# First attention: values of two heads on the two halves of the array, products once per two query tiles, result feature-major

## The reference

```python
def forgetting_attention(q, k, v, f_logit, b_forget):      # 16 heads of 64
    log_f = log_sigmoid(f_logit + b_forget)
    cum = transpose(cumsum(log_f, axis=1), (0, 2, 1))
    for qb in range(4):                                    # query tiles of 128
        s = einsum('bqhd,bkhd->bhqk', q[:, qs:qe], k[:, :qe]) / 8
        s = s + (cum[:, :, qs:qe, None] - cum[:, :, None, :qe])
        p = softmax(where(s_pos <= t_pos, s, -inf))
        outs.append(einsum('bhqk,bkhd->bqhd', p, v[:, :qe]))

o = forgetting_attention(...)
y_att = o.reshape(B, S, 1024) @ w_att_out
m = sigmoid(g_conv) * y_conv + sigmoid(g_att) * y_att
x = x + m @ w_out
```

## Time and profile before

| | |
|---|---|
| median of 3 runs | 1786.18 us (1785.49 to 1787.08) |
| profiled execution | 1786.99 us, its span 1784.9 us |
| TensorE busy | 1715.3 us of the span (96%) |
| VectorE busy | 849.3 us (48%) |
| ScalarE busy | 639.0 us (36%) |
| mean granted TensorE clock | 0.987 |
| first attention, first scores to last product | 274 to 512 us |

### The profile page before, as it was taken

The page is one execution under the profiler, slowest core; times in us unless marked ns, Lnnn a source line. Parts: engine busy times, 40 slices in busy tenths (PEclk is TensorE's granted clock), DMA queues, the critical chain, the costliest instruction groups (busy, mean ns, idle before and its releaser), DMA issues.

```text
span 1784.9 us, 21909 instructions
## 1 busy us (share of the span) xinstructions
PE 1715.3 (96%) x8597; PEld 1251.2 (70%) x8597; DVE 849.3 (48%) x1578; ACT 639.0 (36%) x1102; POOL 96.3 (5%) x131
## 2 busy tenths in 40 slices
PE   6999999999999889999999998899999999999899
PEld 5888888888888744343434433788788888988677
DVE  3544345444565443333333334872647643447782
ACT  4122225444541401111111113754353332457760
POOL 0000001001000000000000000110011000000320
PEclk9999999999999889999999999999999999999999
DMA  6666364653216769999999996233023342313101
GB/s 151 88 102 97 106 95 72 63 62 66 71 64 246 262 265 425 426 427 426 427 427 428 426 426 269 83 118 95 24 71 95 95 151 82 108 59 98 49 1 71
DMA packets 111350, 317.55 MB, mean 178 GB/s; under 512 B 6485, under 2 KB 79957, under 8 KB 98448
## 3 DMA queue, kind: packets, MB, share of 16 engines
q1 hardware_dynamic: 108080, 309.57, 52.6%
q0 software_dynamic: 2160, 3.92, 0.6%
q10 hardware_dynamic: 1008, 2.65, 0.4%
HBM read 313.78 MB, written 6.30 MB: 179 GB/s over the span
## 4 chain that ended last, share of the span: by engine, by line
PE 88%; DVE 4%; ACT 3%; DMA 3%; issue 1%; SPq 0%; DVEq 0%; ACTq 0%; POOL 0%; POOLq 0%
PE bank L1403 14%; PE bank L1405 14%; PE bank L1404 14%; PE bank L1713 11%; PE bank L1739 6%; PE turned L1403 4%; PE turned L1405 4%; PE turned L1404 4%; PE bank L1484 2%; DMA up<-in_w_e_up 2%; PE bank L1586 2%; PE bank L1781 1%; PE turned L1484 1%; PE bank L1726 1%; DMA w_raw<-in_w_in 1%
## 5 line engine op out<-in xcount | busy, mean ns | idle before, releaser
L2031 DVE TENSOR_TENSOR w_lo<-w_raw,w_hi 128x2048 fp32r<-128x2048 f32 (+1 forms) x72 | 156.9, 2179 | 276.7 <-ACT w_hi L887 276.5
L887 ACT ACTIVATE w_hi<-w_raw 128x512 fp32r<-128x512 f32 (+3 forms) x138 | 169.7, 1252 | 284.2 <-DMA w_raw<-in_w_in 99.0
L1713 PE MATMUL bank<-gate,xt 128*64 128x512 f32 x512 | 225.8, 594 | 1.8 <-DMA up<-in_w_e_up 1.8
L1714 PE MATMUL bank<-up,xt 128*64 128x512 f32 x512 | 225.9, 594 | 0.0
L1713 PEld LDWEIGHTS bank<-gate,xt 128*64 128x64 f32 x512 | 68.7, 137 | 140.1 <-issue 140.1
L1403 PE MATMUL bank<-h1T_hi,w_hi 128*128 128x512 f32 x376 | 151.1, 402 | 0.0
L1405 PE MATMUL bank<-h1T_hi,w_lo 128*128 128x512 f32 x376 | 147.4, 392 | 0.0
L1404 PE MATMUL bank<-h1T_lo,w_hi 128*128 128x512 f32 x376 | 146.8, 390 | 0.0
L1739 PE MATMUL bank<-down,hT 128*64 128x512 f32 x256 | 118.3, 605 | 8.8 <-DVE hT L2360 8.8
L887 ACT ACTIVATE y_s<-bank,slot_w 64x512 f32<-64x512 f32 x63 | 43.0, 682 | 220.3 <-PE bank L1740 99.2
L1740 PE MATMUL bank<-down,hT 128*64 128x512 f32 x256 | 118.3, 605 | 0.0
(11 more groups left out here) (704 smaller groups left out, 3863.1 us busy)
## 6 DMA issues: line engine op xcount, KB each, us to landing
down<-in_w_e_down SPq DMA_DIRECT2D x32, 2048.0 KB, 24.1
up<-in_w_e_up SPq DMA_DIRECT2D x30, 2048.0 KB, 26.6
gate<-in_w_e_gate SPq DMA_DIRECT2D x30, 2048.0 KB, 21.6
w_raw<-in_w_in SPq DMA_DIRECT2D x24, 1024.0 KB, 9.7
w_raw<-in_a_w_in SPq DMA_DIRECT2D x20, 1024.0 KB, 5.3
w_raw<-in_w_in SPq DMA_DIRECT2D x16, 512.0 KB, 9.6
w_raw<-in_a_w_out SPq DMA_DIRECT2D x8, 1024.0 KB, 5.0
w_raw<-in_w_conv_out SPq DMA_DIRECT2D x4, 1024.0 KB, 4.9
```

The costliest lines, as they stand in the source:

```text
L887: return nc.scalar.activation(out, in_, ACT.Copy, scale=scale)
L1713: g_ins = pe.matmul(out[0:CAP, :], x, ring_gate[p][:, c, :], start=c == 0, stop=c == KC - 1)
L1714: u_ins = pe.matmul(out[CAP:, :], x, ring_up[p][:, c, :], start=c == 0, stop=c == KC - 1)
L2031: V.tensor_tensor(ring_view(w_lo, n), ring_view(raw, n), ring_view(w_hi, n).bitcast(F32), ALU.subtract)\
```

## The change

Items are counted in another order: two heads of a pair alternate, query tile by query tile (`head_of`, `tile_of`). The probabilities are scaled by VectorE in SBUF, right after exp, and the transposes wait for that (`p_normed`). Every fourth item TensorE does the value products of the last four items (two query tiles of both heads): stationary are 64 columns of `v1`, moving the 128 columns of `pT`; head 0 of the pair writes partitions 0 to 63 of bank 5, head 1 partitions 64 to 127, and bank 5 collects all four query tiles of a pair, feature-major. ScalarE copies the bank to `o1T` once per pair. There are seven `pT` buffers instead of two. The 32 transposes `OT1` are gone; high and low parts are made from `o1T` in SBUF, after the plan.

```diff
--- before.py
+++ after.py
@@ -161,6 +161,16 @@
     return plan
 
 
+def head_of(i):
+
+    return 2 * (i // 8) + i % 2
+
+
+def tile_of(i):
+
+    return i % 8 // 2
+
+
 def outputs_in_order():
 
     o = [("hT", 0, j) for j in range(KC)]
...
@@ -340,7 +348,7 @@
         f_one = temp("f_one", 11, (H1, 512))
         neg = temp("neg", 0, dt=F32R)
         p_t = [temp(f"p_t{b}", b) for b in (1, 2, 3, 4)]
-        pT_t = [temp(f"pT_t{b}", 5 + b, (P, TT, P)) for b in range(2)]
+        pT_t = [temp(f"pT_t{b}", 5 + b, (P, TT, P)) for b in range(7)]
 
         ring_gate = [big("gate0", 4), big("gate1", 2), at("gate2", [P, KC, FE], F32, BASE)]
         ring_up = [big("up0", 5), big("up1", 3), at("up2", [P, KC, FE], F32, BASE + BIG)]
...
@@ -644,6 +652,13 @@
             count = eng.value_load(over[0:1, 16:17], min_val=0, max_val=OVF)
             return count, lambda i: eng.value_load(over[0:1, bass.ds(i, 1)], min_val=0, max_val=NE - 1)
 
+        o1_left, o1_right, o1_copied, o1_split = sem("o1_left"), sem("o1_right"), sem("o1_copied"), sem("o1_split")
+
+        def until_o1(eng, m):
+
+            eng.wait_ge(o1_left, m + 1)
+            eng.wait_ge(o1_right, m + 1)
+
         moe_first = order[("hT", 1, 0)]
 
         def moe_drained(b):
...
@@ -697,7 +712,7 @@
                                  allow_slow_non_contiguous=True).then_inc(sem("gain_row_made"), 16)
                 if n == slice_no[("mix_out", 0, 0)]:
 
-                    until_taken(sp, ("OT1", KC - 1))
+                    sp.wait_ge(o1_split, KC)
                     sp.dma_start(x1_tok[:, :, :], x_v).then_inc(x_back, 16)
                     sp.wait_ge(sem("gain_row_made"), 16)
                     sp.dma_start(g_ffn[:, :], gain_dram.rearrange("d o -> o d").to_broadcast([P, D])).then_inc(sem("g_ffn_loaded"), 16)
...
@@ -1001,16 +1016,14 @@
             split(slice_no[("v1", 0)] + 2, slices1)
             q1_high(0)
             k1_high(0)
-            for i, _, done, now, pt, _ in plan:
+            for i, _, done, now, pt, o in plan:
                 for key, q in now:
                     split_piece(slice_no[key], q)
                 if i is not None:
-                    keys = (i % TT + 1) * P
+                    keys = (tile_of(i) + 1) * P
                     act.wait_ge(sem("max1_made"), i + 1)
                     if i >= 4:
                         act.wait_ge(results, order[("PT1", i - 4)] + 1)
-                    if i >= 8:
-                        until_taken(act, ("O1", i - 8))
                     took(nc.scalar.activation(p_t[i % 4][:, 0:keys], bank_of(("S1", i))[:, 0:keys], ACT.Exp,
                                               bias=neg_max[:, i % 8:i % 8 + 1], accum_out=row_sum[:, i % 8:i % 8 + 1]), ("S1", i))
                 for key in done:
...
@@ -1024,11 +1037,14 @@
                         src = until_made(act, key)
                         took(copy(gattT[:, key[1], :], src[:, :]), key)
                 if pt is not None and pt % 2 == 0:
-                    keys = (pt % TT + 1) * P
+                    keys = (tile_of(pt) + 1) * P
                     src = until_made(act, ("PT1", pt))
-                    if pt >= 2:
-                        act.wait_ge(results, order[("O1", pt - 2)] + 1)
-                    took(copy(pT_t[0][:, 0:pt % TT + 1, :], src[:, 0:keys].rearrange("p (k q) -> p k q", q=P)), ("PT1", pt))
+                    if pt >= 7:
+                        until_o1(act, (pt - 7) // 4 * 2 + 1)
+                    took(copy(pT_t[pt % 7][:, 0:tile_of(pt) + 1, :], src[:, 0:keys].rearrange("p (k q) -> p k q", q=P)), ("PT1", pt))
+                if o is not None and o % 8 == 7:
+                    until_o1(act, o // 2)
+                    copy(o1T[:, o // 8, :], bank[5][:, :]).then_inc(o1_copied, 1)
             split(slice_no[("att_out", 1)], slices1)
 
             def attention(n_items, S, PT, O, p_buf, pT_buf, bias_made, scale, among):
...
@@ -1054,7 +1070,8 @@
                                                   bias=b_, scale=s_, accum_out=row_sum[:, i % 8:i % 8 + 1]), (S, i))
 
             for j in range(KC):
-                evict_hi(("OT1", j), o1T_hi[:, j, :])
+                act.wait_ge(o1_copied, j + 1)
+                copy(o1T_hi[:, j, :], o1T[:, j, :]).then_inc(hi_made, 1)
             for j in range(KC):
                 until_taken(act, ("gatt", j))
                 nc.scalar.activation(gattT[:, j, :], gattT[:, j, :], ACT.Sigmoid).then_inc(sem("gatt_made"), 1)
...
@@ -1574,24 +1591,30 @@
                 for key, g in here:
                     dense_group(key, g)
                 if pt is not None:
-                    until_taken(pe, ("S1", pt))
-                    transposes(("PT1", pt), [(p_t[pt % 4][:, b * P:(b + 1) * P], P) for b in range(pt % TT + 1)])
-                if o is not None:
-                    if o % (4 * TT) == 0:
+                    pe.wait_ge(sem("p_normed"), pt + 1)
+                    transposes(("PT1", pt), [(p_t[pt % 4][:, b * P:(b + 1) * P], P) for b in range(tile_of(pt) + 1)])
+                if o is not None and o % 4 == 3:
+                    j = o // 8
+                    if o % 16 == 3:
                         for tp in range(2):
-                            until_taken(pe, ("v1", o // (4 * TT), tp))
-                    out = open_bank(pe, ("O1", o))
-                    until_taken(pe, ("PT1", o))
-                    for b in range(o % TT + 1):
-                        ins = pe.matmul(out[:, 0:HD1], pT_t[o % 2][:, b, :], v1[:, b, (o // TT) * HD1:(o // TT + 1) * HD1],
-                                        start=b == 0, stop=b == o % TT)
-                    ins.then_inc(results, 1)
-            for i in range(H1 * TT - 8, H1 * TT):
-                until_taken(pe, ("O1", i))
-            for j in range(KC):
-                transposes(("OT1", j), [(o1_tok[:, tt, j * P:(j + 1) * P], P) for tt in range(TT)])
+                            until_taken(pe, ("v1", o // 16, tp))
+                    if o == 3:
+                        pe.wait_ge(drained[5], len([k for k, (at_, _) in place_of.items() if at_ == 5 and order[k] < order[("S1", 0)]]))
+                    elif o % 8 == 3:
+                        pe.wait_ge(o1_copied, j)
+                    for i in range(o - 3, o + 1):
+                        until_taken(pe, ("PT1", i))
+                    for qt in (tile_of(o) - 1, tile_of(o)):
+                        for b in range(qt + 1):
+                            for x in range(2):
+                                h = 2 * j + x
+                                ins = pe.matmul(bank[5][half_rows(x), qt * P:(qt + 1) * P], v1[:, b, h * HD1:(h + 1) * HD1],
+                                                pT_t[(8 * j + 2 * qt + x) % 7][:, b, :], start=b == 0, stop=b == qt)
+                                if b == qt:
+                                    ins.then_inc((o1_left, o1_right)[x], 1)
+            pe.wait_ge(o1_copied, KC)
             for s in range(4):
-                feature_major("att_out", s, lambda j: ("att_out", j), o1T_hi, o1T_lo, chunk_taken("OT1"))
+                feature_major("att_out", s, lambda j: ("att_out", j), o1T_hi, o1T_lo, lambda c: pe.wait_ge(o1_split, c + 1))
             def turn_x1(h, tt):
                 until_taken(pe, ("mix_out", h, tt))
                 transposes(("h2T", h, tt), [(x1_tok[:, tt, (4 * h + c) * P:(4 * h + c + 1) * P], P) for c in range(4)])
...
@@ -2187,13 +2210,20 @@
             split(slice_no[("v1", 0)] + 2, slices1)
             q1_low(0)
             k1_low(0)
+            n_normed = 0
             for i, _, done, now, pt, o in plan:
                 if i is not None:
                     src = until_made(dve, ("S1", i))
                     if i >= 8:
                         until_taken(dve, ("S1", i - 8))
-                    V.tensor_reduce(neg_max[:, i % 8:i % 8 + 1], src[:, 0:(i % TT + 1) * P], AX_X, ALU.max, negate=True)\
+                    V.tensor_reduce(neg_max[:, i % 8:i % 8 + 1], src[:, 0:(tile_of(i) + 1) * P], AX_X, ALU.max, negate=True)\
                         .then_inc(sem("max1_made"), 1)
+                if i != 0 and (i is not None or pt is not None) and n_normed < H1 * TT:
+                    until_taken(dve, ("S1", n_normed))
+                    step(V.reciprocal(inv_sum[:, n_normed % 8:n_normed % 8 + 1], row_sum[:, n_normed % 8:n_normed % 8 + 1]))
+                    p_ = p_t[n_normed % 4][:, 0:(tile_of(n_normed) + 1) * P]
+                    V.tensor_scalar(p_, p_, inv_sum[:, n_normed % 8:n_normed % 8 + 1], None, ALU.mult).then_inc(sem("p_normed"), 1)
+                    n_normed += 1
                 for key, q in now:
                     split_piece(slice_no[key], q)
                 for key in done:
...
@@ -2203,16 +2233,11 @@
                         k1_low(key[1])
                 if pt is not None and pt % 2 == 1:
                     src = until_made(dve, ("PT1", pt))
-                    if pt >= 2:
```

(18 more changed lines are left out.)

14 lines of the change are left out of this document (6 added, 8 removed).

## The result

| | before | after |
|---|---|---|
| median us (runs) | 1786.63 (1785.49 to 1787.82, 4) | 1772.58 (1772.10 to 1773.57, 4) |
| ratio, 95% interval | | 0.9923 (0.9911 to 0.9936) |
| profiled execution, us | 1786.99 | 1772.31 |
| its span, granted clock | 1784.9, 0.987 | 1770.2, 0.985 |

The kernel after is 14.1 us (0.77%) faster. The forecast was 7.8 us faster, 1778.4, and the range ended at 1773.0, 0.4 us above the measured time. The sign and the mechanism held; the gain was taken too small.

The account below looks back on a forecast made before the run. TensorE was taken as the bound. Products, visits and old waits gain 10.9 us, less 0.5 of new waits and 2.6 in the tail: 7.8 faster, 1778.4 us (65%), range 1773 to 1784.

Parts of the forecast that it names:

- the price of before's products: First attention, TensorE value products: 12.6% of 239 us, 30.1 us for 320 records; 29.0 without the last item.
- A pair, 0.11: New value products on two array halves: both run at once, 0.11 us per pair, 146 pairs 16.1 us.
- A visit, 0.34: Going to the array halves and back: 0.20 out and 0.15 in, 0.34 us together; 15 visits 5.1 us.
- Waits: TensorE in the first attention: eight waits of 3.1 us go; 0.5 us of new ones in the last pair of heads.
- The old eight: Gaps before value products in the kernel before, waiting on bank 5 or ScalarE's copy; 3.1 us together.
- The tail: Last transposes to att_out: 8.9 us against 8.78, then 5 us at half clock costing 2.5; 2.6 us lost.
- Halves in turn: Rival for the value products: halves don't overlap, a pair costs 0.22 us; 9.7 us slower, 1795.9; 7%.
- Visits cost nothing: Rival for the value products: visits free and pairs 0.107 us; 13.4 us faster, 1772.8; 13%.
- The hand-over in VectorE: Rival: VectorE's chain late (2 us of waits), visits 0.5 us, clock low twice as long; 3.0 faster, 1783.2; 15%.

Follow-up runs that it names:

- the run with four items per visit: Kernel before, with a head's four query tiles' value products done together every fourth item, old whole-array form, seven pT buffers; 1785.64 us, ratio 0.9992.
- the kernel where VectorE scales first: Kernel before, with VectorE's scaling of the value product, which frees bank 5, ahead of the low parts of q and k; 1783.08 us, ratio 0.9982.
- slice split first: Kernel after, with ScalarE's high parts of the second att_out weight slice made ahead of its last copy of bank 5; 1766.65 us, ratio 0.9889.
- one half: Kernel after, with both heads' products sent to the same half of the array and partitions 0 to 63 of bank 5; 1790.01 us, ratio 1.002.
- both runs on the order of halves: Kernel after, value products head by head instead of alternating: within each query tile, 1776.69 us; within each whole visit, 1782.86 us.

## Why the prediction was right in kind and short in size

- **The step that failed: the price of before's products.** "The chain by line in that window gives the value products (L1586) 12.6%, 239 x 0.126 = 30.1 us" took the chain's share as the price of all 320 records. A chain gives a line only the time that the chain itself spends there, and at six places it runs through ScalarE and VectorE (k_high and k_low in the earlier trace rows) while TensorE works on. One of them, chain of before:

```profile
347.86 0.25 PE bank L1405
...
348.13 0.03 ACT k_high L887
...
352.80 0.41 PE bank L1586 x2
```

and the timeline of the same window, with a whole visit that the chain passes by:

```profile
348.04 1.00 PE L1586 MATMUL bank<-v,pT_t 128*128 128x64 f32 x8
```

  Piece by piece, 46 of the 320 records are left out at these six places. The 30.2 us belong to the other 274, 0.110 each, the price that doubling them measured (33.6 us for 306). So 306 records cost 33.7 us by the chain's own price, not 29.0. With the table's count it is 30.1 and the 5.0 in the transposes' row, 35.1. That is 6.1 of the 7.1 us by which the stretch was short. Of the 1.4 between 33.7 and 35.1, 1.2 would be passages to the products, 62 times the 0.02 of the run with four items per visit. That the table also shows 30.1 for the value products is chance: it is another count, start to start, over 306 records. The forecast had the sign of this in its own text: 0.105 per record times 320 is 33.6, and I took the smaller number without asking why they differ. (It also left the six records of item 62 in the stream, though the tail is counted from the transposes ahead of them: 0.7 us the other way.)
- **A pair, 0.11: right.** 0.109 in after, in the doubled products and in visits of every size. 146 pairs are 15.9 us.
- **A visit, 0.34: right.** 0.16 + 0.18 here, from an expert stage of another shape. The Trainium skill's rule (TensorEngine Tiling (Array Packing), Key Properties) that a change of tiling mode drains TensorE agrees with these numbers. The size was near by luck in part: the forecast took it from products of 512 columns and it had no baseline for what a passage costs without the change of mode (0.08 in before). Products and visits of after together: 18.2 + 15 x 0.17 = 20.8, forecast 21.2; that is 0.4 more of the difference.
- **Dense products took 0.7 us less.** Not forecast. It is spread over the 406 of 512 columns in the body of the groups, under 0.003 us each; why stays open.
- **Waits: right.** The old eight are gone, 3.1 by the rows (six of them tested: 2.45 in the trace for 2.3), new ones about 0.5 at 0.5 forecast, in the last pair of heads as forecast, but for VectorE's copy of pT and not for the scaling.
- **The tail: right, step by step.** 8.87 for 8.9, the clock at half level for 5.25 us (twelve products 0.43 apart) for 5; the end came 2.5 us later after `att_out` for 2.5. Left out was that before's own fall of the clock, under its transposes, also has a price: with the clock at 1.00 that tail takes 7.11 us (the kernel where VectorE scales first).
- **The rivals.** Halves in turn (1795.9) fell: 14 pairs take 1.68 us, and 28 records one by one 3.21. "Visits cost nothing", 1772.8, gave the measured time by the wrong reason: pairs and visits cost what the forecast said, and the 5 us sat on the side of before. The hand-over in VectorE (1783.2) fell. So the time alone would have confirmed the wrong case, and the stretch's count decides.
- **The Trainium skill, TensorE: Matmul & The Clock Gate, Part 3,** lets loads overlap products only with a different row group. The runs disagree: all rows are used by every record here, yet a record on one half takes 0.109, the 0.107 of its 128 moving columns (a quarter of the 0.43 in the earlier trace rows) and next to nothing for its load, and a pair on two halves takes the same 0.109.

## What to carry to other kernels

To price instructions that a change removes, count from start to start on the engine and include what the row ahead of them gains when they go; a line's share of the chain prices only the records through which the chain passes (274 of 320 here), so count them before you divide or multiply, and doubling the instructions is the direct test. Two products on two column halves run at the price of one if they alternate, and still overlap in part within a few records; entering and leaving the halves costs a third of a microsecond, so batch the visits. When a change puts a stage's hand-over into one row of ScalarE and VectorE work, look for what in that row doesn't depend on the last product: here moving one split was worth 5.9 us, over a third of what the change itself brought.

## What was not expected of the hardware

- One change of half in a row of records saves about 0.35 us, a little over three records of 0.109: in these runs the overlap of the halves reaches only that far.
- The granted clock doesn't follow the length of the pause alone. It fell to 0.57 in before behind idle times of 0.57 and 0.78 us (at 513.13 in the timeline); it stayed at 1.00 in the kernel where VectorE scales first, behind 0.58 and 0.77, with the same records between them, and with four items per visit behind 0.87 and 1.25. Behind 0.87 and 2.51 us (slice split first) it stayed at 1.00; behind 0.87 and about 5.6 it was 0.50 in all six traces that have that pause without work in it (after, one half, both runs on the order of halves, one query tile per visit, products of after twice). What decides in the short cases isn't settled by these runs.
